# Forming the modulation rows of the first two column groups on TensorE, in four column groups of its array, in a decoder-layer kernel

## The reference, cut to what matters

```python
c_act = jax.nn.silu(c)                       # c: 1 x 2048
mod = c_act @ w_ada[l] + b_ada[l]            # w_ada: 2048 x 12288
sh1, sc1, gt1, sh2, sc2, gt2 = jnp.split(mod, N_MOD, axis=-1)
h = modulate(rms_norm(x, g_pre_mix[l]), sh1, sc1)   # h * (1 + scale) + shift
proj = h @ w_in[l]                           # 2048 x 5128
```

## Time and profile before

| | |
|---|---|
| median of three runs | 2170.28 us |
| the profiled execution's own time | 2170.66 us |
| its span, first to last instruction | 2168.9 us |
| TensorE busy | 97% of the span |
| VectorE busy | 74% |
| ScalarE busy | 37% |
| mean granted TensorE clock | 0.99 of full |

### The profile page before, as it was taken

The page is one execution under the profiler, slowest core; times in us unless marked ns, Lnnn a source line. Parts: engine busy times, 40 slices in busy tenths (PEclk is TensorE's granted clock), DMA queues, the critical chain, the costliest instruction groups (busy, mean ns, idle before and its releaser), DMA issues.

```text
span 2168.9 us, 25152 instructions
## 1 busy us (share of the span) xinstructions
PE 2107.8 (97%) x9025; PEld 1678.0 (77%) x9025; DVE 1614.6 (74%) x1863; ACT 797.7 (37%) x1035; POOL 99.5 (5%) x105
## 2 busy tenths in 40 slices
PE   5999999999999999999999999999999999999997
PEld 4777778778778777878778778778778787787785
DVE  7998597875977887686686776776866767767766
ACT  5324612224552265243343343343332433433433
POOL 1001050000220001000000000000000000000000
PEclk8999999999999999999999999999999999999999
DMA  9995458845437763322332332333323323323333
GB/s 331 364 288 173 137 185 293 294 162 191 136 131 254 272 215 99 99 96 87 118 100 91 106 97 87 106 98 105 97 95 109 97 87 107 98 92 117 98 122 150
DMA packets 181582, 324.57 MB, mean 150 GB/s; under 512 B 12648, under 2 KB 49624, under 8 KB 179216
## 3 DMA queue, kind: packets, MB, share of 16 engines
q1 hardware_dynamic: 173600, 302.08, 43.1%
q0 software_dynamic: 3568, 16.95, 2.1%
q10 hardware_dynamic: 4352, 4.73, 0.7%
HBM read 313.20 MB, written 10.52 MB: 149 GB/s over the span
## 4 chain that ended last, share of the span: by engine, by line
PE 68%; DVE 16%; issue 7%; ACT 5%; DMA 2%; SPq 1%; DVEq 0%; ACTq 0%
PE pair L834 9%; PE pair L836 9%; PE pair L835 9%; PE pair L859 7%; PE pair L860 7%; PE pair L861 7%; PE bank L526 4%; PE bank L527 4%; PE bank L528 4%; PE bank L536 2%; PE bank L538 2%; PE bank L537 2%; DVE acc L1442 2%; ACT w_hi L1263 2%; DVE w_lo L1414 2%
## 5 line engine op out<-in xcount | busy, mean ns | idle before, releaser
L1862 DVE TENSOR_TENSOR yg<-yg,pair 128x1024 f32<-128x1024 f32 x240 | 289.8, 1218 | 315.6 <-PE pair L861 315.6
L834 PE MATMUL pair<-h_hi,w_lo 128*128 128x512 f32 x1020 | 404.6, 397 | 0.0
L836 PE MATMUL pair<-h_hi,w_hi 128*128 128x512 f32 x1020 | 403.9, 396 | 0.0
L835 PE MATMUL pair<-h_lo,w_hi 128*128 128x512 f32 x1020 | 403.5, 396 | 0.0
L859 PE MATMUL pair<-w_hi,op_lo 128*128 128x512 f32 x840 | 333.4, 397 | 2.3 <-DVE op_lo L1829 2.2
L860 PE MATMUL pair<-w_lo,op_hi 128*128 128x512 f32 x840 | 332.8, 396 | 0.0
L861 PE MATMUL pair<-w_hi,op_hi 128*128 128x512 f32 x840 | 331.9, 395 | 0.0
L964 ACT ACTIVATE w_hi<-raw 128x1024 fp32r<-128x1024 f32 (+1 forms) x114 | 118.7, 1044 | 324.1 <-DMA raw<-in_w_in_dram 201.3
L836 PEld LDWEIGHTS pair<-h_hi,w_hi 128*128 128x128 f32 x1020 | 191.9, 188 | 46.8
L835 PEld LDWEIGHTS pair<-h_lo,w_hi 128*128 128x128 f32 x1020 | 192.0, 188 | 46.4 <-issue 0.2
L834 PEld LDWEIGHTS pair<-h_hi,w_lo 128*128 128x128 f32 x1020 | 191.7, 188 | 46.5 <-issue 0.2
(11 more groups left out here) (272 smaller groups left out, 2781.0 us busy)
## 6 DMA issues: line engine op xcount, KB each, us to landing
raw<-in_w_ada_dram SPq DMA_DIRECT2D x128, 512.0 KB, 4.6
w_raw<-in_w_ff_dram SPq DMA_DIRECT2D x128, 512.0 KB, 3.8
raw<-in_w_ff_dram SPq DMA_DIRECT2D x128, 512.0 KB, 4.5
raw<-in_w_in_dram SPq DMA_DIRECT2D x74, 512.0 KB, 4.7
gst<-in_w_ada_dram SPq DMA_DIRECT2D x64, 512.0 KB, 9.5
raw<-in_w_out_dram SPq DMA_DIRECT2D x32, 512.0 KB, 4.8
x_tok<-in_x_dram SPq DMA_DIRECT2D x4, 1024.0 KB, 8.4
xr<-in_x_dram POOLq DMA_DIRECT2D x4, 1024.0 KB, 7.7
```

The costliest lines, as they stand in the source:

```text
L834: pe.matmul(b, lo[:, cols], h_hi[:, kt, :], start=(kt == 0), stop=False)
L835: pe.matmul(b, hi[:, cols], h_lo[:, kt, :], start=False, stop=False)
L836: last = pe.matmul(b, hi[:, cols], h_hi[:, kt, :], start=False, stop=(kt == KT - 1))
L1862: dve.tensor_tensor(y, y, pairs[2 + (i + r) % 2][:, :, :], ALU.subtract if i == 6 else ALU.add).then_inc(product_read, 1)
```

## The change

`PE_GROUPS = 2`: for groups 0 and 1 VectorE does no `start_sums` at all. In their place:

- `c_rep` (in the memory of `ssq`) holds each of the 16 columns of `c_act` 32 times over, made by one VectorE copy right after `c_act`.
- `weigh_quarter(j, q, bank)` on TensorE multiplies the four rows of a quarter. For each row it issues four float32 matmuls, one for each 32-column group of the array: weights `c_rep[:, k]` (128 x 32), moving operand 128 of the row's 512 numbers, result on partitions 32b to 32b+31 of `bank`, columns 128 to 255. All 16 rows of the group, and the bias in front of them (four matmuls with `ones`), add up in PSUM, so that the sum over rows and over partitions is made there.
- ScalarE copies that 128x128 result into `acc`, and `turn_rows(j)` turns it into four columns with one float32 matmul.
- In TensorE's sequence the quarters 0 to 2 of group 0 stand behind the transposes of `x` and ahead of the transposes of the vector parameters, quarter 3 behind these. Quarters 0 and 1 of group 1 stand between P unit and Q unit of group 0, quarters 2 and 3 behind the Q unit.
- In ScalarE's sequence the copy stands ahead of `hi_part(P_UNIT[j])`, and waits for the group's last quarter.
- The loads that refill `gst` and `acc_init` for groups 1 and 2 wait for `quarter_read` of TensorE. Counts of `row_added` and `sums_added` are shifted for the later groups.

```diff
@@ load_init / start_quarter (SyncE)
+                elif m > PE_GROUPS:
+                    sp.wait_ge(row_added, 16 * (m - 1 - PE_GROUPS) + 1)
                 elif m:
-                    sp.wait_ge(row_added, 16 * (m - 1) + 1)
+                    sp.wait_ge(quarter_read, 4 * (m - 1) + 1)
...
-                if i >= 4:
-                    sp.wait_ge(row_added, 4 * (i - 3))
+                if i >= 4 * (PE_GROUPS + 1):
+                    sp.wait_ge(row_added, 4 * (i - 3 - 4 * PE_GROUPS))
+                elif i >= 4:
+                    sp.wait_ge(quarter_read, i - 3)
@@ TensorE
+            def weigh_quarter(j, q, bank):
+                pe.wait_ge(gst_in[q], 32 * (j + 1))
+                sides = range(4)
+                if q == 0:
+                    pe.wait_ge(init_in, 32 * (j + 1))
+                    for b in sides:
+                        pe.matmul(bank[32 * b:32 * (b + 1), P:2 * P], ones[:, 0:32], acc_init[:, b * P:(b + 1) * P],
+                                  start=True, stop=False, tile_position=(0, 32 * b))
+                for r in range(4):
+                    row = gst[q][:, r].rearrange("p a b -> p (a b)")
+                    for b in sides:
+                        last = pe.matmul(bank[32 * b:32 * (b + 1), P:2 * P], c_rep[:, 4 * q + r, :], row[:, b * P:(b + 1) * P],
+                                         start=False, stop=(4 * q + r == KT - 1), tile_position=(0, 32 * b))
+                last.then_inc(quarter_read, 1)
+            def turn_rows(j):
+                pe.wait_ge(xt_copied, KT + j + 1)
+                pe.matmul(banks[7][:, 0:4], acc[:, j % 2, 0:P], ident[:, 0:P:32], start=True, stop=True).then_inc(acc_read, 1)
             pe.wait_ge(const_ready, 2)
+            pe.wait_ge(xt_copied, 12)
+            for q in range(3):
+                weigh_quarter(0, q, banks[0])
             pe.wait_ge(vec_in, 16 * 9)
             pe.wait_ge(xt_copied, KT)
             pe.transpose(banks[7][:, 0:112], vrow[0:112, :], ident[0:112, 0:112]).then_inc(vec_turned, 1)
+            weigh_quarter(0, 3, banks[0])
             pe.wait_ge(vcol_ready, 1)
-            column_job(0, banks[7])
+            turn_rows(0)
...
             for j in range(8):
-                for n in (P_UNIT[j], Q_UNIT[j]):
+                for i, n in enumerate((P_UNIT[j], Q_UNIT[j])):
                     for k in range(2):
                         first_unit(n, k)
-                if j + 1 < 8:
+                    if j + 1 < PE_GROUPS:
+                        for q in (2 * i, 2 * i + 1):
+                            weigh_quarter(j + 1, q, banks[7])
+                if j + 1 < PE_GROUPS:
+                    pe.wait_ge(mod_read, j + 1)
+                    turn_rows(j + 1)
+                elif j + 1 < 8:
@@ ScalarE
             for j in range(8):
+                if j < PE_GROUPS:
+                    act.wait_ge(quarter_read, 4 * (j + 1))
+                    act.activation(acc[:, j % 2, 0:P], banks[7 * j][:, P:2 * P], ACT.Copy).then_inc(xt_copied, 1)
@@ VectorE
+            step(dve.tensor_copy(c_rep, cc[:, 2, :].unsqueeze(2).to_broadcast([P, KT, 32])))
...
-                for q in range(4):
+                for q in range(4 if j >= PE_GROUPS else 0):
                     start_sums(j, q)
```

More of the change, by code:

```diff
@@ L69, in hybrid_layer @@
     START = [8 * gi - sum(V_FROM[:gi]) for gi in range(9)]
+    PE_GROUPS = 2
     U_LAST = len(FIRST_UNITS)
@@ L199, in hybrid_layer @@
         acc_odd = sq
+        c_rep = ssq[:, :].rearrange("p (k m) -> p k m", m=32)
         gst = [(gst0, gst1)[q // 2][:, q % 2 * 4:q % 2 * 4 + 4] for q in range(4)]
@@ L243, in hybrid_layer @@
         sums_added = sem("sums_added")
+        quarter_read = sem("quarter_read")
         init_in = sem("init_in")
@@ L543, in sums_ready @@
                 if m < 8:
-                    pe.wait_ge(sums_added, m + 1)
+                    pe.wait_ge(sums_added, m + 1 - PE_GROUPS)
                 else:
@@ L1465, in start_sums @@
                     elif k == 1:
-                        if j:
-                            dve.wait_ge(sums_added, j)
+                        if j > PE_GROUPS:
+                            dve.wait_ge(sums_added, j - PE_GROUPS)
                         ins = dve.tensor_scalar(odd, row, c_k, None, ALU.mult)
                     else:
-                        dve.wait_ge(row_added, 16 * j + k - 1)
+                        dve.wait_ge(row_added, 16 * (j - PE_GROUPS) + k - 1)
                         a = odd if k % 2 else even
@@ L1474, in start_sums @@
                 if q == 3:
-                    dve.wait_ge(row_added, 16 * (j + 1))
+                    dve.wait_ge(row_added, 16 * (j + 1 - PE_GROUPS))
                     dve.tensor_tensor(even, even, odd, ALU.add).then_inc(sums_added, 1)
```

## The result

The changed kernel takes 2174.17 us, median of ten runs (2169.41 to 2175.96), and the kernel before, in ten runs beside it, 2169.04 (2165.51 to 2170.95). The ratio is 1.0021, 95% interval 1.0012 to 1.0029: slower by some 4.5 us. The direction was as forecast, the size was not: the prediction said 10.7 us more. The profiled executions have spans of 2173.9 and 2168.9 us. Three executions further down, one of them of the kernel before, took about twice the usual time (4215 to 4444 us) and are left out of the ratios.

The account below looks back on a forecast made before the run. VectorE sets the pace from 60 us on; in the opening, group 1's first matmul moves everything later. Its shift, 120m - 2.18 = +10.7 us, on 2170.66 gave 2181.4, and 0.4 less for the median, 2181.0; range 2173 to 2197.

Parts of the forecast that it names:

- the price of one weighing matmul, m: TensorE's time per weighing matmul in groups 0 and 1: 0.107 us taken, range 0.053 to 0.26.
- The formula: Start of group 1's first matmul: 50.72 + 120m against 52.90 us before, a shift of 120m - 2.18 us.
- The start of group 0: First matmul of group 0 at 33.54 + 52m, 39.1 us with m = 0.107, against 34.56 before.
- Group 0's 42 matmuls: TensorE's unit matmuls of group 0 take 12.35 us, the first twelve at half clock.
- each change between the whole array and its column groups: Emptying TensorE's pipeline: at most 0.17 us, six times on the path, 0 to 1.0; taken as zero.
- The tail: TensorE idle ahead of group 1's first matmul for gap, copy, `hi_part`, `lo_part` and 2.14 us more: together 4.83 us.
- rival (a): Four column groups fully side by side on TensorE, m = 0.053: +4.2, 2174.5 us; chance 0.20.
- freed VectorE time: Groups 0 and 1: the freed 11 us a group become idle time, as group 2's sums stand behind `lo_part(P_UNIT[1])`.
- the shift at group 1's start: Group 1's first matmul comes 10.7 us later with m = 0.107, and this shift is found at the span's end.
- Loads: SyncE's later refills of `gst`, issued 3 to 4 us late, cost nothing; 0 to 2 us in the range.
- The clock: TensorE's clock in groups 0 and 1: taken as zero; up to +5.6, or -2.3 and -1.9, in the range.
- (b): No overlap of weighing matmuls on TensorE, m = 0.21 to 0.26: +23 to +29, 2193.5 to 2199 us; chance 0.30.

Follow-up runs that it names:

- the first experiment: Changed kernel with each row as one float32 matmul of 512 columns on the first 32 array columns, nothing side by side: 2193.66 us against 2170.0 for the kernel before.

## Why the prediction was right in direction and wrong in size

**The step that failed is the price of one weighing matmul, m.** I took 0.107 us, from the thought that the two records of one float32 matmul use one column group, and that matmuls keep their order, so that only two could overlap. Measured: 64 records (32 matmuls) in 1.93 us, 0.053 a matmul at their steps and 0.057 to 0.061 with bias, start and switch. That is four streams at full overlap, the bound that I gave 0.20 to. The Trainium skill's rule on packed matmuls ("TensorE: Matmul & The Clock Gate", "Measured speedup vs the span model") was nearer than my reasoning: the estimate from it was some 0.06. The formula with the measured 0.058 gives 120 x 0.058 - 2.2 = +4.8 at group 1's start; the trace has +3.84 there, and 4.2 at the end of the stage. The time was +4.5 to +5.1.

**The other terms.** The start of group 0 was to be 33.54 + 52m, 36.6 with the measured m. It was 35.12: the transposes of `x` ended near 23.1 and not 24.67, as the profiled execution had the full clock at 20 to 30 us (1.00, against 0.84 before). I had read their end from one trace; in twelve of the fourteen traces here they take 3.9 us and not 5.35. This more than pays for 0.3 us of slower DMA issue on ScalarE (26.46 to 30.52, 4.06 and not 3.75). Group 0's 42 matmuls took 12.97 us (8.55 and 4.42) for 12.35: two more at half clock, and some 0.10 us at each change between the whole array and its column groups (43.34 to 43.67 us where a step is 0.233), which I had set to nothing with 0.17 as the most. The tail was 4.53 from the start of ScalarE's copy, for 4.83 with the gap ahead of it. The weighing of group 1 took 4.12 us for 68 x 0.058 = 3.9. These add up: 35.12 + 12.97 + 4.12 + 4.53 = 56.74. Against the formula's 57.7 they are 0.9 us less, so that the time came out as near to rival (a)'s as it did is in part luck.

**Where the 22 us of freed VectorE time went** was read rightly: idle, as its sums for group 2 stand behind `lo_part(P_UNIT[1])` (16.98 us idle). That the shift at group 1's start is found at the end was right: 3.84 there, 4.22 at groups 2 and 7, 5.0 in the span. The 0.4 between the first two is two more matmuls at half clock. The last 0.8 isn't explained, and little can be read from it: from `take_start` of group 7 to the end the traces of the kernels here take 2012.2 to 2017.3 us, with nothing changed there but the place of the gate loads. One small misreading: the 66 matmuls and the column job leave TensorE 16.91 - 15.4 - 1.0 = 0.5 us of room in a period, not 0.3; it made up nothing either way, as VectorE sets the pace.

**Loads** were right at nothing: no engine but TensorE waited for a quarter, once, 0.58 us, and asking later changed nothing. **The clock** I set to zero, with both ends in the range; it came out slightly against the change (14 and 11 matmuls at half clock for 12 and 9), but by no more than traces differ: in kernels without added matmuls there, 7 to 14 matmuls of group 0 ran at half clock, and 9 to 13 of group 1 where VectorE made its sums. Of the changed kernel's ten executions the two with the highest mean clock (0.994 and 0.993, the others 0.990 to 0.992) are also the two quickest, 2169.41 and 2170.97 us. What I missed is that this term could be moved: 1.6 us less idle time ahead of group 1 kept the clock up. How much idle time lets it fall isn't shown; with 0.94 us ahead of one column job it fell too. **Rival (a)**, four groups side by side, 2174.5, was the outcome; (b) is what the first experiment built on purpose, 2193.7 for the 2193.5 to 2199 written.

## What to carry to other kernels

Before moving work to an engine that is idle now and then, list what stands behind it in that engine's sequence: here 4.1 us of weighing in TensorE's line and a tail of 4.5 us replaced sums that ran beside the units. When only one term of a sum isn't in the trace, and it is multiplied by 120, its value decides everything: give the forecast to the whole interval, or look for a measurement of overlap before choosing the middle. And idle time bought early in a stage is only kept if the loads behind it have room (with the gate loads behind group 3, 2.6 us were lost again; with them behind group 7, nothing).

## What the runs showed of the hardware that was not expected

- Float32 matmuls on four 32-column groups of the array overlap fully, although each is two records on the same group and these stand next to each other: 26.3 ns a step at 128 columns, eleven records under way in 0.05 us, against 107 ns with nothing side by side (0.86 us for a row of 512 columns in two records, the first experiment).
- No floor was met down to 13.7 ns a step at 64 columns. The Trainium skill, "TensorE: Matmul & The Clock Gate", section "Wait — 56ns, not 53.3ns?", has starts never closer than about 25 ns; for matmuls on different column groups the measurement here is below that, and by the rule that the prediction cites from the same page such starts may be some 4 ns apart.
- Matmuls with all weights zero keep the clock up as well: with them ahead of group 1 none of its matmuls ran at half clock, where nine to thirteen did without them in kernels with VectorE's sums. (Only the weights were zero, not the streamed operand.)
- The clock can fall in the middle of a full stage: after 0.94 us of idle time ahead of a column job, eight matmuls ran at half clock (84 to 90 us of the kernel before with added matmuls).
